# Two token-major value units on the unnormalised x open each of the first block's mixers; the exact normalised x is made behind them

## What is computed

```
for l in range(2):
    x = x + 0.5 * swiglu(rmsnorm(x, ffn1_norm[l]), ffn1_w_in[l], ffn1_w_out[l])
    x = x + hybrid_mixer(rmsnorm(x, mix_norm[l]), w_in[l], ...)
    x = x + 0.5 * swiglu(rmsnorm(x, ffn2_norm[l]), ffn2_w_in[l], ffn2_w_out[l])

rmsnorm(x, g) = x * rsqrt(mean(x * x) + 1e-6) * g
hybrid_mixer: h @ w_in is cut into dn_q, dn_k, dn_v, dn_z, dn_b, dn_a, sb_q, sb_k, sb_v, gate_a, gate_b
    q, k, v = silu(causal_conv(dn_qkv)); a gated delta rule over 8 heads in chunks of 64 (g from dn_a, beta from dn_b)
    stick-breaking attention over sb_q, sb_k, sb_v; two gated branches; merged @ w_out
```

## Time and profile before

| | |
|---|---|
| median of 3 runs | 2573.19 us (2572.71 to 2574.45) |
| profiled execution | 2571.15 us |
| its span, first to last instruction | 2569.2 us |
| PE busy | 2423.7 us, 94% |
| PEld busy | 2268.2 us, 88% |
| POOL busy | 1789.0 us, 70% |
| ACT busy | 1116.2 us, 43% |
| DVE busy | 1039.7 us, 40% |
| HBM read | 357.00 MB, 139 GB/s over the span |

### The profile page before, as it was taken

How to read it: one execution, slowest core, us unless ns; L and a number is a source line. 1 busy time by engine, 2 the same in 40 slices (tenths; PEclk the granted TensorE clock), 3 DMA queues, 4 the chain that set the end, 5 groups by cost and what they waited for, 6 DMA issues and landing times.

```text
span 2569.2 us, 44169 instructions
## 1 busy us (share of the span) xinstructions
PE 2423.7 (94%) x17548; PEld 2268.2 (88%) x17548; DVE 1039.7 (40%) x1686; ACT 1116.2 (43%) x1255; POOL 1789.0 (70%) x1368
## 2 busy tenths in 40 slices
PE   8999999998899999999999889999898999899998
PEld 7998888988899999898889889999788998788997
DVE  2224555323322222345554242222524665423765
ACT  4334433446333433444343634335455335455433
POOL 6998444455699899864445667997445997635996
PEclk9999999998999999999999999999899999999999
DMA  6555333323455455442233344564223555313553
GB/s 232 190 171 160 96 99 99 99 90 108 133 188 188 164 196 181 149 151 94 83 99 107 107 132 148 180 203 139 93 96 103 195 183 171 114 64 117 180 185 118
DMA packets 312188, 359.88 MB, mean 140 GB/s; under 512 B 18636, under 2 KB 291072, under 8 KB 311936
## 3 DMA queue, kind: packets, MB, share of 16 engines
q1 hardware_dynamic: 311866, 358.01, 42.8%
q10 hardware_dynamic: 198, 0.06, 0.0%
HBM read 357.00 MB, written 1.05 MB: 139 GB/s over the span
## 4 chain that ended last, share of the span: by engine, by line
POOL 44%; issue 25%; PE 24%; DVE 4%; ACT 2%; POOLq 0%; DMA 0%; ACTq 0%; DVEq 0%
POOL sb_lo L482 44%; PE ps L515 19%; PE ps L579 1%; PE ps L1005 1%; PE ps L981 1%; PE ps L893 1%; ACT sb_sq L1493 0%; DVE sb_negmax L2002 0%; PE ps L566 0%; PE ps L1057 0%; POOLq L489 0%; ACT sb_levels L1466 0%; DMA sb_hcol<-in_dn_a_log 0%; PE ps L988 0%; DVE sb_kT L1947 0%
## 5 line engine op out<-in xcount | busy, mean ns | idle before, releaser
L482 POOL TENSOR_TENSOR sb_lo<-sb_raw,sb_hi 128x512 fp32r<-128x512 f32 x1364 | 1788.8, 1346 | 757.6 <-ACT sb_hi L1102 756.4
L1102 ACT ACTIVATE sb_hi<-sb_raw 128x2048 fp32r<-128x2048 f32 x341 | 652.7, 1915 | 757.9 <-PE ps L515 743.2
L515 PE MATMUL ps<-sb_hT_h,sb_hi 128*128 128x256 f32 x3268 | 948.2, 290 | 32.2 <-DVE sb_qT L1941 6.6
L515 PE MATMUL ps<-sb_hT_h,sb_lo 128*128 128x256 f32 x3268 | 929.6, 284 | 0.0
L515 PE MATMUL ps<-sb_hT_l,sb_hi 128*128 128x256 f32 x3268 | 929.5, 284 | 0.0
L515 PEld LDWEIGHTS ps<-sb_hT_h,sb_hi 128*128 128x128 f32 x3268 | 630.3, 193 | 47.7 <-issue 22.9
L515 PEld LDWEIGHTS ps<-sb_hT_h,sb_lo 128*128 128x128 f32 x3268 | 630.9, 193 | 3.5 <-issue 1.4
L515 PEld LDWEIGHTS ps<-sb_hT_l,sb_hi 128*128 128x128 f32 x3268 | 630.4, 193 | 0.0
L515 PE MATMUL ps<-sb_hi,sb_o_h 128*128 128x512 f32 (+1 forms) x880 | 316.6, 360 | 15.7 <-issue 9.9
L515 PE MATMUL ps<-sb_hi,sb_o_l 128*128 128x512 f32 (+1 forms) x880 | 312.6, 355 | 0.0
L515 PE MATMUL ps<-sb_lo,sb_o_h 128*128 128x512 f32 (+1 forms) x880 | 312.1, 355 | 0.0
(11 more groups left out here) (335 smaller groups left out, 3082.1 us busy)
## 6 DMA issues: line engine op xcount, KB each, us to landing
sb_raw<-in_ffn_w_in SPq DMA_DIRECT2D x88, 1024.0 KB, 5.1
sb_raw<-in_w_in SPq DMA_DIRECT2D x78, 1024.0 KB, 5.2
sb_raw<-in_ffn_w_out SPq DMA_DIRECT2D x44, 1024.0 KB, 4.9
sb_raw<-in_ffn_w_up SPq DMA_DIRECT2D x44, 1024.0 KB, 5.0
sb_raw<-in_ffn_w_down SPq DMA_DIRECT2D x22, 1024.0 KB, 4.9
sb_raw<-in_w_out SPq DMA_DIRECT2D x16, 1024.0 KB, 5.2
sb_raw<-in_w_branch_a SPq DMA_DIRECT2D x8, 1024.0 KB, 5.0
sb_raw<-in_w_branch_b SPq DMA_DIRECT2D x8, 1024.0 KB, 5.1
```

The source lines that it names most:

```text
L482: ins = nc.gpsimd.tensor_tensor(lo[:, slot, c], raw[:, slot, c], hi[:, slot, c].bitcast(F32), ALU.subtract)
L515: ins = mm(dst, s, m, start=first and n == 0, stop=last and n == 3 * len(pairs) - 1)
L1102: fn(hi[:, slot, :], raw[:, slot, :], ACT.Copy).then_inc(hi_ready, 1)
```

## The change

1. The entry of both mixers of the first block is rebuilt after the pattern of `enter`. The first FFN of each layer turns two pairs of blocks of x ahead of the last piece of its last down product (`next_n`, `lows`). x without its root, times the gain, goes to `o_h`, `o_l`, with the blocks moved round by 4 (`UNSCALED_AT`), since the lower blocks of `o_h`, `o_l` still hold that product's operands. `scaled`, `transposes`, `high`, `low` and `stats` are gone from this place, with the 20 warm-up transposes.
2. The mixer's order begins with sv0 and sv1. They are multiplied token-major from `o_h`, `o_l` (`unscaled_part`, in halves of four blocks each, so that the second pair of turns lies between them), and ACT applies the root of each token as it evacuates them into `tok`.
3. The exact normalised x is made behind them from the same PSUM banks: DVE multiplies turned x, gain and row into `exact` (which is `qT`), ACT copies this to `hT_h`, DVE subtracts into `hT_l` from SBUF. q0 is the first unit that reads it and waits for it pair by pair.
4. `FIRST` becomes sv0, sv1, q0, z0, b, k0, a, v0, q1: q1 is moved out of the first delta stage, which has 5 units instead of 6. From the unit behind it on, the numbers and banks of all units are as before.
5. ACT and DVE have their steps in the order of the new units; ACT makes the splits of units 3 to 10 between them. PE's 16 small matmuls of line 851 stand behind q1 instead of behind q0.
6. The other edits renumber counters (`rstd_ready`, `row_ready`, `diag_ready`, `xn_ready`).

```diff
-FIRST = [("b", 0), ("a", 0), ("sv", 0)] + pair_units(0) + [("sv", 1)]
-DELTA_BG = [pair_units(1) + [("sv", 2), ("sv", 3)], pair_units(2) + [("sq", 0), ("sk", 0)],
+FIRST = [("sv", 0), ("sv", 1), ("q", 0), ("z", 0), ("b", 0), ("k", 0), ("a", 0), ("v", 0), ("q", 1)]
+B_AT, A_AT = FIRST.index(("b", 0)), FIRST.index(("a", 0))
+DELTA_BG = [pair_units(1)[1:] + [("sv", 2), ("sv", 3)], pair_units(2) + [("sq", 0), ("sk", 0)],
...
+            def unscaled_part(b, k, bank, q, k0, k1):
+
+                if k0 == 0:
+                    arrived(b, k)
+                w = weights(k, KB, 256)
+                for t in range(ST):
+                    tt_ = slice(t * P, (t + 1) * P)
+                    for c in range(k0, k1):
+                        if t == 0 and c % 2 == 0:
+                            pe.wait_ge(h_ready, 4 * q + (c // 2 + 1))
+                        for n, (o, wt) in enumerate(((o_h, w[0]), (o_l, w[0]), (o_h, w[1]))):
+                            ins = mm(ps[:, bank, t * S:(t + 1) * S], o[:, (c + UNSCALED_AT) % KB, tt_], wt[:, c, :],
+                                     start=(t, c, n) == (0, 0, 0), stop=(c, n) == (KB - 1, 2), skip_group_check=True)
+                if k1 == KB:
+                    ins.then_inc(unit_done, 1)
...
             def mixer1(l, b, q):
+                unscaled_part(b, 0, 0, q, 0, 4)
+                pe.wait_ge(x_ready, updates(q))
+                for g in range(2, 4):
+                    turn(g, AFTER_FFN_BANKS[g])
+                unscaled_part(b, 1, 1, q, 0, 4)
+                turn_row(3 * l + 1, AFTER_FFN_ROW)
+                unscaled_part(b, 0, 0, q, 4, KB)
+                unscaled_part(b, 1, 1, q, 4, KB)
+                pe.wait_ge(bank_free[0], BANK_UNITS[0] * l + 1)
+                arrived(b, 2)
+                wh, wl = weights(2, KB, 256)
+                for k0, k1 in ((0, 4), (4, KB)):
+                    for i in range(2):
+                        for c in range(k0, k1):
+                            if i == 0 and c % 2 == 0:
+                                pe.wait_ge(exact_low, 4 * l + (c // 2 + 1))
...
+                ins.then_inc(unit_done, 1)
                 pe.wait_ge(start_loaded, 16)
-                for r in range(4):
-                    unit1(l, b, r, None if r else q)
+                for r in range(3, len(FIRST)):
+                    unit1(l, b, r)
                 pe.wait_ge(rows_dve, ROWS_DVE.at(l, "beg"))
...
-                for r in range(4, len(FIRST)):
-                    unit1(l, b, r)
                 warm(2)
...
-                ffn(2 * l, b, sil_ready, 2 * NCH * l)
-                transposes(3 * l + 1, l)
+                ffn(2 * l, b, sil_ready, 2 * NCH * l, 3 * l + 1)
                 mixer1(l, b + NCH, 3 * l + 1)
...
                 if kind == "sv":
                     dst = tok[:, :, S * c:S * (c + 1)]
+                    if c < 2:
+                        act.wait_ge(unit_done, RING * b_of(l) + (r + RING + 1))
+                        for t in range(ST):
+                            ins = fn(dst[:, t, :], v[:, t, :], ACT.Copy, scale=rstd[:, t:t + 1])
+                        ins.then_inc(bank_free[bank], 1)
+                        return
...
-            def mixer1(l, b):
+            def mixer1(l, b, gain):
+                q = 3 * l + 1
+                split(b, 0)
+                split(b, 1)
+                for g in range(2):
+                    high_pair(q, g, gain, o_h, AFTER_FFN_BANKS[g], UNSCALED_AT)
+                squares(q)
+                for g in range(2, 4):
+                    high_pair(q, g, gain, o_h, AFTER_FFN_BANKS[g], UNSCALED_AT)
+                diagonal()
                 split(b, 2)
-                act.wait_ge(unit_done, RING * b + (0 + RING + 1))
-                fn(beta_r[:, :], ps[0:HEADS, 0, 0:S], ACT.Exp, scale=-1.0).then_inc(bank_free[0], 1)
-                split(b, 3)
-                freed(l, 1)
+                take_row(q, AFTER_FFN_ROW)
+                for g in range(4):
+                    act.wait_ge(exact_ready, 4 * l + (g + 1))
+                    sl = slice(2 * g, 2 * g + 2)
+                    fn(hT_h[:, sl, :], exact[:, sl, :], ACT.Copy).then_inc(exact_high, 1)
+                    if g == 1:
+                        evac1(l, 0)
+                        split(b, 3)
+                evac1(l, 1)
+                split(b, 4)
+                split(b, 5)
+                evac1(l, 3)
+                split(b, 6)
+                act.wait_ge(unit_done, RING * b + (B_AT + RING + 1))
+                fn(beta_r[:, :], ps[0:HEADS, B_AT % 2, 0:S], ACT.Exp, scale=-1.0).then_inc(bank_free[B_AT % 2], 1)
+                split(b, 7)
+                split(b, 8)
+                freed(l, A_AT)
...
                 fn(e, e, ACT.Ln, bias=1.0).then_inc(rows_act, 1)
+                split(b, 9)
...
-                plain(l, b, range(2, len(FIRST) - 1))
                 split(b, len(FIRST) + 1)
                 pre_squares(l, 0)
...
+                dve.wait_ge(row_ready, 3 * l + 2)
+
+                def exact_pair(g):
+                    for i in range(2):
+                        k = 2 * g + i
+                        ins = stt(out=exact[:, k, :], in0=ps[:, AFTER_FFN_BANKS[g], i * S:(i + 1) * S], scalar=vec1[:, V1_MIX + k:V1_MIX + k + 1],
+                                  in1=row[:], op0=ALU.mult, op1=ALU.mult)
+                    ins.then_inc(exact_ready, 1)
+
+                exact_pair(0)
+                for g in range(4):
+                    if g < 3:
+                        exact_pair(g + 1)
+                    dve.wait_ge(exact_high, 4 * l + (g + 1))
+                    c = slice(2 * g, 2 * g + 2)
+                    tt(hT_l[:, c, :], exact[:, c, :], hT_h[:, c, :].bitcast(F32), ALU.subtract).then_inc(exact_low, 1)
                 dve.wait_ge(start_loaded, 16)
-                dve.wait_ge(unit_done, RING * b + (1 + RING + 1))
-                ts(y, ps[h8, 1, 0:S], hcol[:, 0:1], None, ALU.add).then_inc(bank_free[1], 1)
-                freed(l, 0)
+                evac1(l, b, 2)
+                evac1(l, b, 5)
+                dve.wait_ge(unit_done, RING * b + (A_AT + RING + 1))
+                ts(y, ps[h8, A_AT % 2, 0:S], hcol[:, 0:1], None, ALU.add).then_inc(bank_free[A_AT % 2], 1)
...
                 tt(y, beta_r[:, :], eg_r[:, :], ALU.mult).then_inc(rows_dve, 1)
+                evac1(l, b, 7)
                 dve.wait_ge(rows_pe, l + 1)
...
-                for r in range(2, len(FIRST)):
-                    evac1(l, b, r)
+                evac1(l, b, 8)
                 pre_norm(l, 0)
```

More of the change, by code:

```diff
@@ L289, in build_program @@
         diag = tok[:, 0, 0:S]
+        exact = qT
         junk = kT[:].rearrange("p (t k) n -> p t (k n)", t=ST)
@@ L1120, in high_pair @@
                     k = 2 * g + i
-                    ins = fn(dst[:, k, :], ps[:, bank, i * S:(i + 1) * S], ACT.Copy, scale=gain(k))
+                    ins = fn(dst[:, (k + at) % KB, :], ps[:, bank, i * S:(i + 1) * S], ACT.Copy, scale=gain(k))
                 ins.then_inc(hh_ready, 1)
@@ L1596, in low_pair @@
                     k = 2 * g + i
-                    ins = stt(out=dst_l[:, k, :], in0=ps[:, bank, i * S:(i + 1) * S], scalar=gain(k), in1=dst_h[:, k, :].bitcast(F32),
+                    to = (k + at) % KB
+                    ins = stt(out=dst_l[:, to, :], in0=ps[:, bank, i * S:(i + 1) * S], scalar=gain(k), in1=dst_h[:, to, :].bitcast(F32),
                               op0=ALU.mult, op1=ALU.subtract)
```

62 lines of the change are left out of this document (31 added, 31 removed).

## The result

| | before | after |
|---|---|---|
| median | 2573.59 us of 4 runs (2572.71 to 2574.45) | **2603.15 us** of 4 runs (2602.27 to 2604.76) |
| ratio | | 1.0113, interval 1.0095 to 1.0131 |
| span of the profiled execution | 2569.2 us | 2600.5 us |
| PE busy | 2423.7 us | 2434.6 us |
| DVE busy | 1039.7 us | 1115.1 us |

The account below looks back on a forecast made before the run. With PE 94% busy, only its waits were taken as movable. Per mixer, `pre` 5.77 us later less 4.7 from the delta stage gave +1.1, +2.1 for both: median 2575.3 us, range 2568.0 to 2581.0.

Parts of the forecast that it names:

- PE waits for POOL ahead of v0: In the mixer's head, v0 needs POOL's low half 7, so PE was to wait 1.7 us.
- `pre` starts: End of the mixer's head: `pre` at 266.35, 5.77 us later than before, with 5.76 us of q1 done.
- The timing of the entry: Start of the mixer: sv0 and sv1 done at 221.3, q0 at 229.4, three units' matmuls 3.2 us earlier.
- the second layer's hand-over: The hand-over ahead of the second layer's first FFN, taken as the new entry's model with 677.77 us subtracted.
- POOL's pace: Low halves in the mixer's head: 5.46 us each for 2 and 3, 5.01 for 4 and 5.
- the chain is 8.96 long: DVE's small steps from a to the last of line 1856, in the head: 247.7 to 256.7, length as before.
- The rival on the shared port: Mixer's head: four DVE subtractions hold POOL up 2.76 us in all; +1.7 a mixer, 2578.7 us, chance 0.13.
- PE's wait ahead of `pre`: End of the mixer's head: PE was to wait some 2 us for ACT's squares.
- The first delta stage's return: With q1 moved out, the stage was to get 4.7 us shorter, less than q1's 5.76.
- my lower bound: The least that the first delta stage was to give back: 2.9 us.
- the third rival: First delta stage gives back only 2.9 us, q1 having filled waits; +2.9 a mixer, 2579.0 us, chance 0.13.
- Twice the first mixer: Both mixers' heads taken as alike, one worked out and counted twice: +1.1 us each, +2.1 for both.

Follow-up runs that it names:

- e2: The changed kernel with POOL waiting for its own last result ahead of each unit of its loop; 2584.67 us.
- e14: The changed kernel with POOL's pause ahead of every third unit only, those in slot 1; 2583.99 us.
- e9: e2 with 40 instead of 20 warm-up transposes of PE ahead of `pre` in layer 1's mixers; 2579.49 us.
- e5: e3 with the changed kernel's order of units alone, the old entry kept and q1 out of the first delta stage; 2582.00 us.
- e3: The kernel before with POOL waiting for its own last result ahead of each unit of its loop; 2569.47 us.
- e4: The kernel before with beta made wholly on ACT, without DVE's addition and reciprocal; 2573.91 us.

## Why the prediction was wrong, point by point

In us; after is given less 3.06, e2 plus 0.96 (the second pair of blocks of its sv0 stands at 208.37).

| step | forecast | after | e2 |
|---|---|---|---|
| sv0, sv1 done | 221.3 | 221.7 | 221.7 |
| q0 done | 229.4 | 228.9 | 229.0 |
| PE waits for POOL ahead of v0 | 1.7 | 1.15 | 1.38 |
| the same ahead of k0 | 0 | 1.13 | 1.38 |
| DVE evacuates a | 247.7 | 248.4 | 248.8 |
| chain of small steps, length | 8.96 | **15.44** | 9.26 |
| `pre` starts | 266.35 | **273.6** | 267.7 |
| `pre` takes | 1.98 | 3.48 | 1.98 |
| first delta stage against 71.21 | −4.7 | −4.05 | −3.9 |

- **The timing of the entry was right** to 0.5 us: the second layer's hand-over was a fair model for the first mixer. DVE's subtractions took 1.24, 0.99 and 1.25; the forecast took 1.67 and kept 0.69.
- **POOL's pace** was right, and its effect on PE was in two places instead of one. The two waits take 2.3 us of the 3.7 that q0 is earlier than before (232.6 against 228.9), where the forecast had 1.7 of 3.2; the chain takes the rest.
- **The step that failed is "the chain is 8.96 long".** I read it from a place where DVE was let in between POOL's instructions and moved it to one where it was not. In after it is 15.44 long, 6.5 us more, and that goes straight into `pre`, which starts 7.2 us later than forecast. It is not the only one: without the holds e2 still measured 2584.67, above the range, and the next points are about that. The rival on the shared port had the right two engines but the wrong side of the trade: it priced what DVE costs POOL (2.76 us), and the cost was what POOL costs DVE (10 us in one instruction). The Trainium skill ("SBUF — State Buffer", section "SBUF: two separate sides") says that, for the kinds of VectorE instruction that need the shared pair of ports, whichever of the two engines starts first keeps the pair "for the whole instruction; the other fully blocks". The trace agrees with a wait of up to one instruction (1.24 and 1.46 where 0.69 and 0.33 are free of it); the 10.09 us is eight instructions of POOL, more than the rule says, and there the measurement decides. The same section speaks of deep queues that would have to be drained to share the pair. The ends of the holds, each just behind a gap in POOL's run, fit that, those of e14 too; that other instructions were let in with no gap near doesn't.
- **Half-rate time was left out.** I added PE's wait ahead of `pre`, 2 us, at its own length. In after, `pre` took 3.48 and the granted clock was 0.59 for the 13 us ahead of it; in the second mixer `pre` took 3.7 and the first delta stage 70.81 at 0.92, where the first mixer's took 67.16 at 1.00. That longer waits bring this on is argued, not shown. For it: in e9, with the wait of the second mixer filled, the window behind `pre` is at 1.00 instead of 0.50. Against it: e2 and e5 wait the same 2.3 us in both mixers, and only in the second does the clock fall.
- **The first delta stage's return was mis-sized.** −4.05 in after looks near −4.7, but on kernels with the same pauses it is 70.20 to 67.31, −2.9, which is my lower bound and the third rival's figure; and in the second mixer of e5 and e2 it is +0.9 and +0.5, with the half-rate stretch in it.
- **"Twice the first mixer" failed.** Up to the end of the first mixer's delta work e5 is 5.0 us behind e3, by the end of the second mixer 12.4, and over the whole 14.8. The same edit met another state of the clock the second time. The last 3 us or so are in the second block, where the code is the same: one stretch (from 2222.61 in e3, from 2235.59 in e5) takes 26.37 us at a clock of 0.87 in e3 and 28.28 at 0.70 in e5. Without the holds the first mixer is near the forecast: by the splits e2 loses 2.1 us in it against the kernel before (forecast 1.1), in the second 6.9, and 3.7 behind both.
- **Outside the changed code** I had nothing. The hold at 47.21 us is in code that the change doesn't touch, and four more are in the second block: about 9 us together by the splits. Holds of this kind in unchanged code come with e4's small edit too, so they can't be read off the code.
- **The chances** of the rivals add up to 0.67 for the same and 0.19 for slower, not 0.65 and 0.21; it changes nothing here.

The sum as it came: 18.5 us with the holds and what follows them (e2 against after), 12.5 by the medians or 9 by the ratios for the order alone (e5 against e3), 2.7 by the medians or 5 by the ratios for the entry on top (e2 against e5), less the 4 us that the pauses give on the kernel before. What stays open: the condition under which DVE is kept out of a run of POOL, what makes the clock fall behind one wait and not behind an equal one, and how much of the 15 us between e2 and e3 is clock and how much is order.

## What to carry to other kernels

A chain of small instructions has the length that it had in its old place only if its neighbours stay the same. The trace of the kernel before could not have warned: its longest DVE instruction is under 2.8 us. So before moving such a chain beside a GpSimd run without a gap, give a rival the price of one instruction held to the end of that run, and in the new trace look for the longest instruction of each form, not its mean. A pause in GpSimd's loop is a cheap remedy to try. And ahead of a stage that is bound by PE, an idle stretch can cost more than its length: behind the same 2.3 us wait e5 lost 4.5 us at half rate in `pre` and the first delta stage of the second mixer, and nothing in the first. Read the granted clock behind each wait before counting it at its own length.
